# Input tile by input tile instead of chunk by chunk, for the first two weight chunks of a stage

## The chip, the cores and the metric

One core of one Trainium2 chip runs the whole program. The metric is the device time of one launch in microseconds (us). PE is the matrix engine (TensorE), DVE the vector engine, ACT the scalar engine, POOL is GpSimd, SP issues transfers.

## The reference, cut to what matters

One inference step of a decoder trunk of two layers, for 512 prompt tokens and 8 sample tokens that share all weights. Layer 0 mixes tokens by sparse attention, layer 1 by a causal pooling. All of it is float32:

```
x <- LN(ALPHA*x + 0.5*SwiGLU_1(x));  x <- LN(ALPHA*x + mixer(x));  x <- LN(ALPHA*x + 0.5*SwiGLU_2(x))

def _layernorm(x, g, b):
    mu = jnp.mean(xf, axis=-1, keepdims=True)
    var = jnp.mean(jnp.square(xf - mu), axis=-1, keepdims=True)
    y = (xf - mu) * lax.rsqrt(var + LN_EPS) * g + b

def _swiglu(x, w_i, w_o):
    h = jnp.einsum('btd,df->btf', x, w_i)
    gate, up = h[..., :D_FF], h[..., D_FF:]
    return jnp.einsum('btf,fd->btd', jax.nn.silu(gate) * up, w_o)
```

D_MODEL is 1024 and D_FF is 2816. A projection (`x @ w_in`, 2120 columns) comes before the attention.

## The kernel before, in words

The activations stay in SBUF with the features on the partitions: `xf` is 8 tiles of 128 features by 520 tokens. The tokens are handled in two halves of 260 (`HT`, `cols(h)`). A matmul keeps float32 accuracy in three products: every operand is split into a rounded high part and the remainder, `xh` and `xl` for the activations, `w_hi` and `w_lo` for the weights, and the products are xh*w_hi, xh*w_lo and xl*w_hi.

The seven stages are, in order, `f0` (feed-forward), `pr` (projection and attention), `op` (output projection), `f1`, `f2` (feed-forward), `pl` (pooling mixer), `f3` (feed-forward). The weights come in chunks of 1 MB: 8 tiles of 128 input features (k) by two blocks of 128 output columns (m). SP loads a chunk into `w_raw`, ACT makes `w_hi` (L486), DVE makes `w_lo` (L1155); each has two buffers. PE multiplies in `products` (L770). Each chunk has four banks of PSUM, two blocks m by two halves h: even chunks have banks 0 to 3, odd ones 4 to 7.

Five stages begin with `two_chunks`: f0, pr, f1, f2 and f3. It runs chunk 0 and chunk 1 for the first half of the tokens, then both for the second half. For one half and chunk, `products` first goes over the 8 tiles of `xh` with w_hi and w_lo (8 x 2 x 2 = 32 matmuls), then over the 8 tiles of `xl` with w_hi (16 matmuls). So a half has 2 x 48 = 96 matmuls. Chunk 0 waits before each tile of `xh` and each tile of `xl` for the semaphores `s_xh` and `s_x`; chunk 1 finds them all there.

Each engine runs its own list of instructions in order. What comes before `two_chunks` (except in f0) is the layer norm of the stage before, in `tail`. For the half h: PE sums with a matrix of means (`stats`, L813, six float32 matmuls, each of which the trace shows as two), ACT copies the mean (L499) and squares it (L500), DVE makes the variance and its reciprocal (L1170 to L1174), ACT takes the root (L504), DVE subtracts and multiplies tile by tile (L1181, L1187). Then `affine` on ACT writes per tile `xh` (L517) and then `xf` (L522), and POOL writes `xl` = xf - xh (L1765). `stats` of half 0 runs in the stage before. `stats` of half 1 is the function `left`, which the next stage gets as `middle_0`: it runs in the middle of the first 32 matmuls of chunk 0, at k = 4. All of the layer norm of half 1, and with it `xh` and `xl` for the second half of `two_chunks`, follows from it.

In f0 there is no layer norm ahead: all tiles of `xh` and `xl` come from the loaded input (ACT L720, POOL L1747), and `left` is None.

Of the kernel before, what the change touches and what calls it, by code (L numbers as in the profile page):

```python
# [18 lines left out]
KD = D // P  # L19
# [3 lines left out]
HT = TOK // 2  # L23
# [79 lines left out]
def trunk_kernel(nc, a, outs, stages):  # L103
    ctx = ExitStack()
    with ctx:
        def sem(name):
            return ctx.enter_context(nc.semaphore(name))
# [4 lines left out]
        def at(name, shape, dt=F32, offset=None):  # L112
            size = int(np.prod(shape[1:])) * (2 if dt == BF16 else 4)
            if offset is None:
                offset = top[0]
                top[0] += -(-size // 64) * 64
            return nc.alloc_sbuf_tensor_at(name, shape, dt, offset=offset)
# [3 lines left out]
        xh = at("xh", [P, KD, TOK], F32R)  # L121
        xl = at("xl", [P, KD, TOK], F32R)
# [3 lines left out]
        w_hi = at("w_hi", [P, 2, CHUNK], F32R)  # L126
        w_lo = at("w_lo", [P, 2, CHUNK], F32R)
# [27 lines left out]
        ps = ctx.enter_context(nc.psum_tensor("ps", [P, 8, 512], F32))  # L155
# [95 lines left out]
        def cols(h):  # L251
            return slice(h * HT, (h + 1) * HT)
# [10 lines left out]
        s_hi = sem("s_hi")  # L263
        s_lo = sem("s_lo")
        s_used = sem("s_used")
        s_free = sem("s_free")
# [12 lines left out]
        s_xh = sem("s_xh")  # L279
        s_xf = sem("s_xf")  # L280
        s_x = sem("s_x")
# [199 lines left out]
        def _(act):  # L481
# [47 lines left out]
            def proj(name):  # L529
                st = plan[name]  # L530
                act.dma_start(rope[:], a["c_rope"]).then_inc(s_rope_in, 16)
                act.wait_ge(s_kept, 32)
                act.wait_ge(s_stat, 2)
                act.dma_start(kidx[:], keys_dram.rearrange("n h (t d) -> (h t) n d", d=IDX_DIM)).then_inc(s_pages, 16)
                for li, (kind, g, _) in enumerate(PROJ):
                    if 1 <= li < len(PROJ) - 1:
                        if PROJ[li + 1][0] == "ki":
                            act.wait_ge(s_kiw, 16)
                        split_hi(st.chunk + li + 1)
                    act.wait_ge(s_used, 2 + st.chunk + li + 1)  # L540
                    for m, x in enumerate(rotated(li)):
                        nc.scalar.activation(halves(x), ps[:, 4 * (li % 2) + 2 * m:4 * (li % 2) + 2 * m + 2, 0:HT],
                                             ACT.Copy).then_inc(s_praw, 1)
# [208 lines left out]
        def _(pe):  # L752
            def products(c, nk, bank, hi, lo, first, last, m_cols=(P, P), before_hi=None, before_lo=None, middle=None,
                         only=(0, 1)):

                wh = w_hi[:, c % 2, 0:nk * 256].rearrange("p (k u c) -> p k u c", k=nk, u=2)
                wl = w_lo[:, c % 2, 0:nk * 256].rearrange("p (k u c) -> p k u c", k=nk, u=2)
                for x, before, ws in ((hi, before_hi, (wh, wl)), (lo, before_lo, (wh,))):  # L760
                    for k in range(nk):
                        if before is not None:
                            before(k)
                        if middle is not None and x is hi and k == nk // 2:
                            middle()
                        for m in range(2):
                            mc = m_cols[m]
                            for w in ws:
                                for h in only:
                                    mm = nc.tensor.matmul(ps[0:mc, bank + 2 * m + h, 0:HT], w[:, k, m, 0:mc],  # L770
                                                          x(k)[:, h * HT:(h + 1) * HT],
                                                          start=first and k == 0 and w is wh and x is hi,
                                                          stop=last and k == nk - 1 and x is lo)
                if 1 in only:
                    mm.then_inc(s_used, 1)
                return mm

            def first_x(st, h):

                return 0 if st.x == KD else st.x - 2 * KD + KD * h  # L780

            def two_chunks(st, middle_0, middle_1):

                for h in range(2):
                    for j in range(2):
                        if h == 0:
                            pe.wait_ge(s_lo, st.chunk + j + 3)
                            pe.wait_ge(s_free, 2 * (st.group + j) + 2)
                        products(st.chunk + j, KD, 4 * j, x_hi, x_lo, True, True,
                                 before_hi=(lambda k: pe.wait_ge(s_xh, first_x(st, h) + k + 1)) if j == 0 else None,  # L790
                                 before_lo=(lambda k: pe.wait_ge(s_x, first_x(st, h) + k + 1)) if j == 0 else None,
                                 middle=middle_0 if (h, j) == (0, 0) else middle_1 if (h, j) == (1, 1) else None, only=(h,))

            def x_hi(k):
                return xh[:, k, :]
# [20 lines left out]
            def ffn(name, left):  # L816

                st = plan[name]
                two_chunks(st, left, None)
                with pe.Fori(0, KF // 2 - 1) as i:  # L820
                    for j in (2, 3):
# [38 lines left out]
            def proj(name, left):  # L860
                st = plan[name]
                two_chunks(st, left, lambda: rotate(0))
                for li, (kind, g, _) in enumerate(PROJ):
                    if li < 2:
                        continue
                    c = st.chunk + li
                    pe.wait_ge(s_lo, c + 3)
                    pe.wait_ge(s_free, 2 * (st.group + li) + 2)
                    products(c, KD, 4 * (li % 2), x_hi, x_lo, True, True,
                             m_cols=(P, IDX_HEADS) if kind == "ki" else (P, P), middle=lambda: rotate(li - 1))  # L870
# [927 lines left out]
```

## Time and profile before

| what | value |
|---|---|
| time, median of 3 runs | 2199.44 us (2195.97 to 2200.57) |
| the profiled execution's own time | 2196.03 us |
| its span | 2194.2 us |
| PE busy | 1994.8 us, 91% of the span |
| DVE, ACT, POOL busy | 874.2, 597.8, 466.6 us |
| mean granted clock of PE | 0.936 of full speed |
| share of PE in the chain that ended last | 78% |

The span is what the profiler saw of the program; the time holds 1.8 us around it. PE is busy nearly everywhere but in the attention (about 540 to 860 us) and at the seams between stages. The seams that this change touches begin at 416 us (pr), 910 us (f1), 1302 us (f2) and 1775 us (f3); f0 begins its matmuls at 31.85 us.

### The profile page before, as it was taken

The page shows a single profiled execution, that of the slowest core. Times are in us where ns is not written, and L with a number is a line of the kernel's source. Part 1 is how long each engine was busy: PE and PEld are TensorE (multiplying, and loading weights), DVE is VectorE, ACT ScalarE, POOL GpSimd, SP SyncE. Part 2 cuts the span into 40 slices and gives each one's busy share as a digit, 9 for nine tenths or more (in the row PEclk, how much of TensorE's full clock was granted, in tenths as well). Part 3 has the DMA queues.
Part 4 walks back from the last instruction along what each step waited for, and adds up shares of the span by engine and source line. Part 5 has one row for each costly group of instructions (what it writes and reads, how often), then busy time and mean ns, then how long its engine had stood idle before and what let it go on. Part 6 is the DMA issues. An engine that isn't in the chain of part 4 may idle for free.

```text
span 2194.2 us, 36231 instructions
## 1 busy us (share of the span) xinstructions
PE 1994.8 (91%) x15486; PEld 1906.1 (87%) x15486; DVE 874.2 (40%) x1228; ACT 597.8 (27%) x837; POOL 466.6 (21%) x408
## 2 busy tenths in 40 slices
PE   6999999999957677999999999999999379999996
PEld 5999999999645456899999989999998369999996
DVE  2333322543686622533332244333224653333223
ACT  2222122421214241522222133122123452122123
POOL 2211121300000063511111232111121651111120
PEclk9999999999559798999999999999999689999998
DMA  5453322251000032233332232332230123323321
GB/s 168 139 168 96 96 87 87 74 157 39 23 0 1 1 87 68 77 96 88 84 96 87 92 92 78 96 89 83 91 106 30 51 69 96 96 83 89 98 77 39
DMA packets 258364, 179.55 MB, mean 82 GB/s; under 512 B 10806, under 2 KB 254782, under 8 KB 257757
## 3 DMA queue, kind: packets, MB, share of 16 engines
q1 hardware_dynamic: 248368, 153.71, 24.0%
q10 hardware_dynamic: 7797, 11.98, 1.7%
q0 software_dynamic: 2112, 12.59, 1.6%
q8 instruction: 67, 1.10, 0.2%
q14 instruction: 20, 0.16, 0.0%
HBM read 169.57 MB, written 8.08 MB: 81 GB/s over the span
## 4 chain that ended last, share of the span: by engine, by line
PE 78%; DVE 6%; issue 6%; ACT 3%; POOL 3%; another core or an unknown queue 1%; DMA 1%; ACTq 0%; POOLq 0%; DVEq 0%
PE ps L770 74%; PE ps L813 2%; PE ps L905 1%; DVE iwork L1310 1%; DVE best L1307 1%; ACT w_hi L486 1%; DVE w_lo L1155 1%; POOL diag L1706 1%; DVE xf L1181 1%; POOL sum_sq L1650 1%; DVE xf L1187 1%; POOL sum_z L1648 1%; ACT xf L522 1%; POOL k_sel L1696 1%
## 5 line engine op out<-in xcount | busy, mean ns | idle before, releaser
L770 PE MATMUL ps<-xh,w_hi 128*128 128x260 f32 x3264 | 684.7, 286 | 39.3 <-ACT xh L517 17.1
L770 PE MATMUL ps<-xh,w_lo 128*128 128x260 f32 x3264 | 677.2, 284 | 0.0
L1155 DVE TENSOR_TENSOR w_lo<-w_raw,w_hi 128x2048 fp32r<-128x2048 f32 (+2 forms) x153 | 441.0, 2883 | 442.5 <-ACT w_hi L486 442.5
L770 PEld LDWEIGHTS ps<-xh,w_hi 128*128 128x128 f32 x3264 | 519.4, 190 | 45.7 <-issue 26.6
L770 PEld LDWEIGHTS ps<-xh,w_lo 128*128 128x128 f32 x3264 | 519.8, 190 | 0.7
L770 PE MATMUL ps<-xl,w_hi 128*128 128x260 f32 x3264 | 411.7, 283 | 1.3 <-POOL xl L1734 1.3
L770 PEld LDWEIGHTS ps<-xl,w_hi 128*128 128x128 f32 x3264 | 399.6, 188 | 2.0 <-POOL xl L1734 1.5
L486 ACT CAST w_hi<-w_raw 128x2048 fp32r<-128x2048 f32 (+2 forms) x153 | 282.0, 1844 | 274.1 <-PE ps L770 262.9
L770 PE MATMUL ps<-hh,w_hi 128*128 128x260 f32 x1408 | 293.0, 283 | 0.0
L770 PE MATMUL ps<-hh,w_lo 128*128 128x260 f32 x1408 | 291.4, 282 | 0.0
L1580 DVE TENSOR_TENSOR hid<-silu_g,ps 128x520 f32<-128x520 f32 x88 | 61.3, 696 | 547.4 <-ACT silu_g L683 514.8
L683 ACT ACTIVATE silu_g<-ps 128x520 f32<-128x520 f32 x88 | 53.3, 605 | 758.5 <-PE ps L770 758.5
L770 PEld LDWEIGHTS ps<-hh,w_lo 128*128 128x128 f32 x1408 | 224.1, 188 | 0.1
L770 PEld LDWEIGHTS ps<-hh,w_hi 128*128 128x128 f32 x1408 | 223.9, 188 | 0.1
L1658 POOL CAST hh<-hid 128x520 f32 (+1 forms) x88 | 54.7, 621 | 787.9 <-DVE hid L1580 787.9
L770 PE MATMUL ps<-hl,w_hi 128*128 128x260 f32 x1408 | 177.5, 282 | 0.0
L770 PEld LDWEIGHTS ps<-hl,w_hi 128*128 128x128 f32 x1408 | 172.1, 188 | 0.0
L1660 POOL TENSOR_TENSOR hl<-hid,hh 128x520 f32 (+1 forms) x88 | 115.6, 1314 | 14.2 <-POOL hh L1658 14.1
L1648 POOL TENSOR_TENSOR sum_z<-sum_z,xf 128x520 f32<-128x520 f32 x36 | 58.3, 1619 | 200.3 <-DVE xf L1163 196.6
L1765 POOL TENSOR_TENSOR xl<-xf,xh 128x260 fp32r<-128x260 f32 x64 | 70.5, 1119 | 100.5 <-ACT xf L522 100.1
L1706 POOL TENSOR_TENSOR diag<-const,row_inv 128x512 f32<-128x512 f32 x16 | 16.7, 1042 | 336.3 <-DVE row_inv L1498 335.9
L970 PE MATMUL ps<-kd,q_t 64*128 64x512 f32 (+3 forms) x128 | 41.1, 609 | 31.6 <-DVE row_max L1438 31.6
(243 smaller groups left out, 1373.1 us busy)
## 6 DMA issues: line engine op xcount, KB each, us to landing
w_raw<-in_ffn_wi_dram SPq DMA_DIRECT2D x176, 512.0 KB
w_raw<-in_ffn_wo_dram SPq DMA_DIRECT2D x32, 1024.0 KB
w_raw<-in_ffn_wo_dram SPq DMA_DIRECT2D x16, 768.0 KB
w_raw<-in_attn_w_in_dram SPq DMA_DIRECT2D x8, 1024.0 KB
keys_scratch<-key_half POOLq DMA_DIRECT2D x2, 2048.0 KB, 7.9
w_raw<-in_attn_w_o_dram SPq DMA_DIRECT2D x4, 1024.0 KB
x_in<-in_x_prompt_dram ACTq DMA_DIRECT2D x1, 2048.0 KB
out_dram<-y_out ACTq DMA_DIRECT2D x4, 512.0 KB
```

The lines of the kernel that those rows point to most:

```text
L486: nc.scalar.copy(w_hi[:, c % 2, 0:n], w_raw[:, c % 2, 0:n]).then_inc(s_hi, 1)
L683: nc.scalar.activation(halves(silu_g[:, j % 2, :]), ps[:, 4 * (j % 2):4 * (j % 2) + 2, 0:HT], ACT.Silu).then_inc(s_silu, 1)
L770: mm = nc.tensor.matmul(ps[0:mc, bank + 2 * m + h, 0:HT], w[:, k, m, 0:mc], x(k)[:, h * HT:(h + 1) * HT], start=first and k == 0 and w is ...
L813: mm = nc.tensor.matmul(ps[:, 2 * q + h, 0:HT], mean_ones, x[:, cols(h)], start=n == 0, stop=n == 2)
L970: nc.tensor.matmul(ps[:, H % 2, 0:(i + 1) * P], q_t[64 * e:64 * e + 64, h // 2, i * P:(i + 1) * P], kd[64 * e:64 * e + 64, g, 0:(i + 1) * ...
L1155: nc.vector.tensor_tensor(w_lo[:, c % 2, 0:n], w_raw[:, c % 2, 0:n], w_hi[:, c % 2, 0:n].bitcast(F32), ALU.subtract).then_inc(s_lo, 1)
L1580: nc.vector.tensor_tensor(halves(hid[:, j % 2, :]), halves(silu_g[:, j % 2, :]), ps[:, b + 2:b + 4, 0:HT], ALU.mult).then_inc(s_free, 2)
L1648: nc.gpsimd.tensor_tensor(sum_z[:], sum_z[:], xf[:, d, :], ALU.add).then_inc(s_sum, 1)
L1658: nc.gpsimd.tensor_copy(hh_ij, hid[:, j:j + 1, :]).then_inc(s_hh, 1)
L1660: nc.gpsimd.tensor_tensor(hl_ij, hid[:, j:j + 1, :], hh_ij.bitcast(F32), ALU.subtract).then_inc(s_hl, 1)
L1706: nc.gpsimd.tensor_tensor(diag[:, B % 2], ident.unsqueeze(1).broadcast_to([P, 4, P]), row_inv[:, B % 2, :].unsqueeze(2).broadcast_to([P, 4 ...
L1765: nc.gpsimd.tensor_tensor(xl[:, d, cols(h)], xf[:, d, cols(h)], xh[:, d, cols(h)].bitcast(F32), ALU.subtract).then_inc(s_x, 1)
```

## The change

`two_chunks` no longer calls `products` for the first half of the tokens, but a new function `first_half`. It goes over the input tiles: for each k it multiplies `xh` with w_hi and w_lo of chunk 0 and with w_hi of chunk 1 (6 matmuls), then the `xl` of the tile before with w_hi of both chunks (4 matmuls). w_lo of chunk 1 comes after all tiles (16 matmuls). The second half of the tokens is as before. `left` is called at the same k = 4, after the six `xh` matmuls of that tile.

```
-                for h in range(2):
-                    for j in range(2):
-                        if h == 0:
-                            pe.wait_ge(s_lo, st.chunk + j + 3)
-                            pe.wait_ge(s_free, 2 * (st.group + j) + 2)
-                        products(st.chunk + j, KD, 4 * j, x_hi, x_lo, True, True,
-                                 before_hi=(lambda k: pe.wait_ge(s_xh, first_x(st, h) + k + 1)) if j == 0 else None,
-                                 before_lo=(lambda k: pe.wait_ge(s_x, first_x(st, h) + k + 1)) if j == 0 else None,
-                                 middle=middle_0 if (h, j) == (0, 0) else middle_1 if (h, j) == (1, 1) else None, only=(h,))
+            def first_half(st, middle):
+                view = "p (k u c) -> p k u c"
+                wh = [w_hi[:, (st.chunk + j) % 2, :].rearrange(view, k=KD, u=2) for j in range(2)]
+                wl = [w_lo[:, (st.chunk + j) % 2, :].rearrange(view, k=KD, u=2) for j in range(2)]
+
+                def tile(j, w, x, k, start, stop):
+                    for m in range(2):
+                        nc.tensor.matmul(ps[:, 4 * j + 2 * m, 0:HT], w[j][:, k, m, :], x[:, k, cols(0)], start=start, stop=stop)
+
+                pe.wait_ge(s_lo, st.chunk + 3)
+                pe.wait_ge(s_free, 2 * (st.group + 1) + 2)
+                for k in range(KD + 1):
+                    if k < KD:
+                        pe.wait_ge(s_xh, first_x(st, 0) + k + 1)
+                        tile(0, wh, xh, k, k == 0, False)
+                        tile(0, wl, xh, k, False, False)
+                        if k == 0:
+                            pe.wait_ge(s_hi, st.chunk + 2)
+                        tile(1, wh, xh, k, k == 0, False)
+                    if k == KD // 2 and middle is not None:
+                        middle()
+                    if k >= 1:
+                        pe.wait_ge(s_x, first_x(st, 0) + k)
+                        tile(0, wh, xl, k - 1, False, k == KD)
+                        tile(1, wh, xl, k - 1, False, False)
+                pe.wait_ge(s_lo, st.chunk + 4)
+                for k in range(KD):
+                    tile(1, wl, xh, k, False, k == KD - 1)
+
+                first_half(st, middle_0)
+                for j in range(2):
+                    products(st.chunk + j, KD, 4 * j, x_hi, x_lo, True, True,
+                             before_hi=(lambda k: pe.wait_ge(s_xh, first_x(st, 1) + k + 1)) if j == 0 else None,
+                             before_lo=(lambda k: pe.wait_ge(s_x, first_x(st, 1) + k + 1)) if j == 0 else None,
+                             middle=middle_1 if j == 1 else None, only=(1,))
```

Only PE's list changes. Its first rows of stage pr before (a row is an instruction or several alike, L770 is the matmul of `products`; in brackets the semaphores that it waits for):

```order
L770 MATMUL ps<-xh,w_hi 128x260 [waits s_xh,s_free,s_lo]
L770 MATMUL ps<-xh,w_lo 128x260
L770 MATMUL ps<-xh,w_hi 128x260
L770 MATMUL ps<-xh,w_lo 128x260
L770 MATMUL ps<-xh,w_hi 128x260 [waits s_xh]
```

The first rows of the same stage in the changed kernel (L791 is the matmul of `first_half`), up to the first tile of `xl`:

```order
L791 MATMUL ps<-xh,w_hi 128x260 [waits s_xh,s_free,s_lo]
L791 MATMUL ps<-xh,w_hi 128x260
L791 MATMUL ps<-xh,w_lo 128x260 x2
L791 MATMUL ps<-xh,w_hi 128x260 [waits s_hi]
L791 MATMUL ps<-xh,w_hi 128x260
L791 MATMUL ps<-xh,w_hi 128x260 [waits s_xh]
L791 MATMUL ps<-xh,w_hi 128x260
L791 MATMUL ps<-xh,w_lo 128x260 x2
L791 MATMUL ps<-xh,w_hi 128x260 x2
L791 MATMUL ps<-xl,w_hi 128x260 [waits s_x]
L791 MATMUL ps<-xl,w_hi 128x260 x3
```

The first wait for `s_x` stands after 12 matmuls now; before, it stood after 32 matmuls and the six of `stats`. The second place is `stats` of half 1 in the same stage. Before, from tile k = 3 on (L813 is `stats`):

```order
L770 MATMUL ps<-xh,w_hi 128x260 [waits s_xh]
L770 MATMUL ps<-xh,w_lo 128x260
L770 MATMUL ps<-xh,w_hi 128x260
L770 MATMUL ps<-xh,w_lo 128x260
L813 MATMUL ps<-sum_z,const 128x260 [waits s_sum,s_xh]
L813 MATMUL ps<-xf,const 128x260 [waits s_free] x2
L813 MATMUL ps<-sum_sq,const 128x260
L813 MATMUL ps<-silu_g,const 128x260 [waits s_sq] x2
L770 MATMUL ps<-xh,w_hi 128x260
```

In the changed kernel, from the `xl` matmuls behind tile k = 3 on (L841 is `stats` there):

```order
L791 MATMUL ps<-xl,w_hi 128x260 [waits s_x]
L791 MATMUL ps<-xl,w_hi 128x260 x3
L791 MATMUL ps<-xh,w_hi 128x260 [waits s_xh]
L791 MATMUL ps<-xh,w_hi 128x260
L791 MATMUL ps<-xh,w_lo 128x260 x2
L791 MATMUL ps<-xh,w_hi 128x260 x2
L841 MATMUL ps<-sum_z,const 128x260 [waits s_sum]
L841 MATMUL ps<-xf,const 128x260 [waits s_free] x2
L841 MATMUL ps<-sum_sq,const 128x260
L841 MATMUL ps<-silu_g,const 128x260 [waits s_sq] x2
```

Before, 16 matmuls stand ahead of `stats`, and no wait for `xl`; now 42 stand ahead of it (6 + 10 + 10 + 10 + 6), and three waits for `xl`.

## Rows read from the trace of the kernel before

**Rows 1.** Page, costliest groups: busy us, mean ns, idle before and its releaser.
```profile
L770 PE MATMUL ps<-xh,w_hi 128*128 128x260 f32 x3264 | 684.7, 286 | 39.3 <-ACT xh L517 17.1
```
**Rows 2.** Waits of PE at four seams: 410 to 425, 905 to 920, 1297 to 1312, 1769 to 1784 us.
```profile
PE ps L770 <- ACT xh L517: 3.0, 2, 2.6
...
PE ps L770 <- ACT xh L517: 3.6, 3, 2.6
...
PE ps L770 <- ACT xh L517: 3.7, 3, 2.6
...
PE ps L770 <- ACT xh L517: 6.6, 2, 6.2
```
**Rows 3.** Timeline of PE at the start of pr: start us, duration us.
```profile
416.45 0.56 PE L770 MATMUL ps<-xh,w_hi 128*128 128x260 f32 x1 [2.64 <-ACT xh L517]
...
417.02 0.42 PE L770 MATMUL ps<-xh,w_hi 128*128 128x260 f32 x1
417.23 0.42 PE L770 MATMUL ps<-xh,w_lo 128*128 128x260 f32 x1
```
**Rows 4.** Timeline of POOL: the first `xl` tile at each seam, and all eight in pr.
```profile
416.88 5.96 POOL L1765 TENSOR_TENSOR xl<-xf,xh 128x260 fp32r<-128x260 f32 x1 [29.09 <-ACT xf L522]
...
416.88 10.91 POOL L1765 TENSOR_TENSOR xl<-xf,xh 128x260 fp32r<-128x260 f32 x8 [29.09 <-ACT xf L522]
...
910.39 5.96 POOL L1765 TENSOR_TENSOR xl<-xf,xh 128x260 fp32r<-128x260 f32 x1 [9.85 <-ACT xf L522]
...
1302.34 5.96 POOL L1765 TENSOR_TENSOR xl<-xf,xh 128x260 fp32r<-128x260 f32 x1 [29.09 <-ACT xf L522]
...
1775.23 5.61 POOL L1765 TENSOR_TENSOR xl<-xf,xh 128x260 fp32r<-128x260 f32 x1 [11.91 <-ACT xf L522]
```
**Rows 5.** Timeline of DVE in pr: the last multiplications of half 0 and what follows.
```profile
419.28 0.76 DVE L1187 TENSOR_TENSOR xf<-xf,hid 128x260 f32<-128x260 f32 x2
419.96 2.29 DVE L1155 TENSOR_TENSOR w_lo<-w_raw,w_hi 128x2048 fp32r<-128x2048 f32 x1
```
**Rows 6.** Timeline of PE: `stats` at full clock with its end, then the first matmul after `stats` at each seam.
```profile
402.88 0.60 PE L813 MATMUL ps<-sum_z,const 128*128 128x260 f32 x2
...
405.32 0.47 PE L770 MATMUL ps<-hh,w_hi 128*128 128x260 f32 x1
...
424.62 0.48 PE L770 MATMUL ps<-xh,w_hi 128*128 128x260 f32 x1
...
918.83 0.48 PE L770 MATMUL ps<-xh,w_hi 128*128 128x260 f32 x1
...
1311.08 0.47 PE L770 MATMUL ps<-xh,w_hi 128*128 128x260 f32 x1
...
1783.05 0.47 PE L770 MATMUL ps<-xh,w_hi 128*128 128x260 f32 x1
```
**Rows 7.** Timeline of PE in pr: the last group of the first half, and the first matmul of the second.
```profile
432.49 2.08 PE L770 MATMUL ps<-xl,w_hi 128*128 128x260 f32 x16
434.41 0.29 PE L770 MATMUL ps<-xh,w_hi 128*128 128x260 f32 x1
```
**Rows 8.** Timelines: in pr ACT's last `xh` of half 1 and PE's first matmul with it; the same matmul in f2.
```profile
437.12 0.60 ACT L517 ACTIVATE xh<-xf,lnp 128x260 fp32r<-128x260 f32 x1
...
437.77 0.39 PE L770 MATMUL ps<-xh,w_hi 128*128 128x260 f32 x1
...
1324.63 0.39 PE L770 MATMUL ps<-xh,w_hi 128*128 128x260 f32 x1 [0.24 <-ACT xh L517]
```
**Rows 9.** PE in stretches: us, busy (instructions), granted clock, share of DMA, GB/s.
```profile
409.70:416.40 6.70, 4.11 (x35) 1.00 0.23 48
416.50:423.20 6.70, 6.33 (x21) 0.50 0.23 34
423.40:430.00 6.60, 6.60 (x52) 1.00 0.50 157
911.50:918.10 6.60, 5.81 (x18) 0.50 0.13 34
918.30:925.00 6.70, 6.70 (x54) 1.00 0.41 116
```
**Rows 10.** Timeline of f0's start: POOL's eight `xl` tiles, and PE's first matmul of the stage.
```profile
25.44 10.07 POOL L1747 TENSOR_TENSOR xl<-xf,xh 128x520 fp32r<-128x520 f32 x8 [8.49 <-ACT xh L720]
...
31.85 0.39 PE L770 MATMUL ps<-xh,w_hi 128*128 128x260 f32 x1 [0.85 <-DVE xf L1621]
```

## The prediction

> **What bounds the kernel now.** I read the page first. PE is busy for 91% of the span and is 78% of the chain that ended last, so what counts is the time in which PE does nothing or runs slowly. The costliest group shows where its matmuls on `xh` stood idle: 39.3 us in all, 17.1 of them until ACT had written `xh` [rows 1]. Then the waits at the four seams with a layer norm. They are 3.0, 3.6, 3.7 and 6.6 us, and the longest wait of each (2.6, 2.6, 2.6, 6.2) is the one before the first tile [rows 2]. A new order of the matmuls can't shorten that one: at that time there is no tile. What is left between the tiles is 0.4 + 1.0 + 1.1 + 0.4 = 2.9 us over the four seams. That is all that an order "as the tiles come" can fill.
>
> Then I looked at when the other inputs come. POOL's first `xl` tile takes 5.96 us (5.61 in f3), while all eight take 10.91, so that the other seven take (10.91 - 5.96) / 7 = 0.71 each [rows 4]. The first begins at 416.88 and ends at 422.84. In that time DVE multiplies tiles and then makes `w_lo`, until 419.96 + 2.29 = 422.25 [rows 5]; POOL gets going as DVE stops. In the kernel before nobody feels this, because PE comes to `xl` only after `stats`, 424.62 us, and 16 matmuls more [rows 6].
>
> Last, the clock. From 416.5 to 423.2 it is granted at 0.50 (1.2 GHz), from 423.4 on at 1.00 (2.4 GHz); in f1 it is 0.50 from 911.5 to 918.1 [rows 9]. Ahead of the fall in pr PE had stood still for 2.64 us [rows 3].
>
> **The prices.** At full clock 16 matmuls take 434.41 - 432.49 = 1.92 us, 0.12 each [rows 7]. At half clock one takes 0.21 [rows 3]. `stats` at full clock takes 405.32 - 402.88 = 2.44 us [rows 6].
>
> **The change part by part.** No instruction is added or removed but semaphore waits: both orders have 96 matmuls in the first half. What changes is what stands behind what.
>
> *The wait for the first xl.* In pr PE starts at 416.45 and does the 12 matmuls of tiles 0 and 1 at 0.21 each, to 419.0. Then it waits for `xl` tile 0 until 422.84, about 3.8 us. Behind it on PE's list stand the `xh` tiles 2 to 7, which ACT goes on delivering, and `stats`. Later `xl` tiles come each 0.71 us and PE needs at least 10 x 0.12 = 1.2 us for a tile, so there is one such wait per seam.
>
> *The delay of stats, at full clock.* From the first `xl` on, 4 + 10 + 10 + 6 = 30 matmuls (3.60 us) and `stats` (2.44) make 6.04 us. So `stats` would end at these times, against the first matmul after it in the kernel before [rows 4, 6]:
> - pr: 422.84 + 6.04 = 428.88 against 424.62, 4.26 later
> - f1: 916.35 + 6.04 = 922.39 against 918.83, 3.56 later
> - f2: 1308.30 + 6.04 = 1314.34 against 1311.08, 3.26 later
> - f3: 1780.84 + 6.04 = 1786.88 against 1783.05, 3.83 later
>
> The sum is 14.9 us. The 2.9 us of small waits are inside these numbers, since they are taken from absolute times.
>
> *Does it reach the end?* Yes, by the last `xh` of half 1. In pr ACT ends it at 437.12 + 0.60 = 437.72 and PE takes it up at 437.77, and in f2 PE already waits 0.24 us for it [rows 8]. All of the second layer norm hangs on `stats`, by a fixed chain on ACT and DVE, so this tile comes as much later as `stats` does, and there is at most 0.1 us of slack. PE itself would reach the second half at 428.88 + 54 x 0.12 = 435.4, only 1 us later than now (434.41 [rows 7]); it then waits inside the second half. Where 28 matmuls took it to tile 7 by 438.7, the tile comes at 437.72 + 4.3 = 442.0: 3.3 us of new waiting.
>
> *The clock after the first stall.* The clock is at half when PE gets its `xl`, and it now has done little before. Bounds: it could be full at once (0), or come back only as long after PE's restart as before, 416.45 to 423.3 or 6.8 us [rows 3, 9], which costs half of that, 3.4. It is work at half clock in all of these rows after a stall, so I take 4.5 us at half, a cost of 2.2 per seam.
>
> *The clock in the second half.* 3.3 us of waiting in some 6.6 us. Before, the stretch with 4.11 us busy of 6.70 was followed by the fall [rows 9]. This is as thin, but the waits are short ones between tiles. Bounds 0 and 3.4, as above; I take 1.5 per seam.
>
> *At nothing.* Chunk 1's w_lo is wanted later than before and w_hi of chunk 1 is written by ACT ahead of `xh`. The wait for both chunks' banks at the start is for DVE work that lies ahead of the normalising. In f0, POOL's tiles end 1.26 us apart from 26.7 on, the last at 35.5; PE starts at 31.85 and comes to `xl` tile j at 31.85 + (12 + 10 j) x 0.12 = 33.3 + 1.2 j, always later [rows 10]. If POOL were 7 us later there, it would be another such stall. The second half's own order, SP's and POOL's queues are as before. Behind the seams the feed-forward stages have PE busy all the time and pr leads into a chain of dependent work, so nothing there gives the delay back.
>
> **The sum:** 14.9 + 4 x 2.2 + 4 x 1.5 = 29.7 us. Against the profiled execution's own 2196.0 that is 2225.7. The median of the runs is 3.4 us higher, 2199.4, so I say 2229. With both clock terms at nothing it is 14.9 us (2214), with both at their upper bound 14.9 + 27.2 = 42.1 (2241.5).
>
> **The rivals.**
> - *Not slower: the xl tiles are there in time.* The wait at the 13th matmul decides: if POOL ended its first tile by 419.0, in 2.1 us instead of 5.96, PE would run through, and the 2.9 us between the tiles would be filled: 2196.5. For it: POOL's later tiles take 0.71 us. Against it: DVE's work of that time is the same in both kernels and POOL's first tile is long at all four seams [rows 4]. Even so `stats` would stand behind 26 more matmuls. Chance 0.07.
> - *The delay is hidden in the second half.* If the layer norm of half 1 had slack, only the end of the first half would count. After `stats` come 54 matmuls (6.5 us) instead of 80 (9.6), so 3.1 of each delay is made good and 14.9 - 12.4 = 2.5 us are left, with the first clock term 11.3: 2211. Against it stands the 0.24 us wait in f2 [rows 8]. Chance 0.07.
> - *The alternation of banks slows PE.* In the new order each matmul goes to another bank than the one before. If that held PE to 0.21 a matmul, 96 x 0.09 x 5 stages = 43 us would come on top: 2272. Against it: the 16 `xl` matmuls of [rows 7] alternate between two banks at 0.12 each. Chance 0.03. The Trainium skill, page "TensorE: Matmul & The Clock Gate", section "A second HAM failure mode: psum-queue depth-cycling", speaks for it: it tells of a kernel that cycled through PSUM banks and whose clock swung between the two levels by small pauses. By that rule the time would be this rival's; the trace's alternating matmuls at full clock don't bear it out.
>
> **How the numbers follow.** The forecast, a stall for `xl` and a late `stats` that both reach the end, has 0.83. It spans 2214 to 2241.5; I take 2210 to 2243, which lets the hidden case in as well and leaves out the first and the third rival. A measurement of this kernel can tell about 0.2%, 4.4 us, from no change. Faster by more than that: 0.02, a part of the first rival. Within: 0.06, the rest of it and a little of the second. Slower: 0.92.
>
> **What would show it right or wrong.** Right: at pr, f1, f2 and f3 the waits of PE show `xl` <- POOL (L1765) with 3.5 to 5 us each, a new line; small waits for `xh` in the first half go, and new ones of about 3 us per seam for `xh` come in the second half; `stats` ends 3.3 to 8 us later after the first `xh` than before; the half-clock stretch after each seam is longer or comes twice, and the mean granted clock falls below 0.936. POOL's first `xl` still takes near 6 us, and f0 is unchanged. Wrong: no wait for `xl`, or one under 2 us; or the waits as told but the second half unchanged in its end, which is the second rival; or steady matmuls in `first_half` at more than 0.12 us with the clock at 1.00, the third.

## The result, and the profile after

| | kernel before | changed kernel |
|---|---|---|
| median of 5 runs | 2199.44 us | 2224.31 us |
| lowest to highest | 2195.35 to 2200.57 | 2216.84 to 2224.49 |
| span of the profiled execution | 2194.2 us | 2222.5 us |
| mean granted clock of PE | 0.936 | 0.928 |

The changed kernel is slower: ratio 1.0106, 95% interval 1.0085 to 1.0128, which is 23.3 us (18.7 to 28.2) on 2199.4. The ratio is taken over all runs and not from the two medians, which lie 24.9 us apart. The forecast was 2229, 29.7 us above before, with a range of 2210 to 2243.

The waits of PE in the changed kernel, over the whole program (us in total, times, the longest); L791 is the matmul of `first_half`, L770 that of `products`:

```profile
PE ps L791 <- POOL xl L1793: 14.9, 4, 4.5
...
PE ps L791 <- ACT xh L517: 14.1, 4, 6.2
...
PE ps L770 <- ACT xh L517: 7.3, 16, 0.6
```

The first line is new: four waits for `xl`, one per seam, 14.9 us. The second is the wait before the first tile, 2.6 + 2.6 + 2.6 + 6.2, which was there before; the small ones between the tiles of half 0 [rows 2] are gone. The third is new but for one wait of 0.24 us that the kernel before had in f2 [rows 8]: 16 small waits for `xh` in the second half.

The timeline of PE at the start of pr in the changed kernel, from the first matmul to `stats` (L841), the first matmul after it, and the last wait of the second half; it answers to [rows 3] and [rows 6 to 8]:

```profile
418.65 0.59 PE L791 MATMUL ps<-xh,w_hi 128*128 128x260 f32 x2 [2.64 <-ACT xh L517]
...
420.76 0.64 PE L791 MATMUL ps<-xh,w_hi 128*128 128x260 f32 x2
425.08 1.24 PE L791 MATMUL ps<-xl,w_hi 128*128 128x260 f32 x4 [3.68 <-POOL xl L1793]
...
430.57 0.60 PE L841 MATMUL ps<-sum_z,const 128*128 128x260 f32 x2
...
432.32 1.04 PE L841 MATMUL ps<-silu_g,const 128*128 128x260 f32 x4
433.01 0.84 PE L791 MATMUL ps<-xl,w_hi 128*128 128x260 f32 x4
...
446.11 0.39 PE L770 MATMUL ps<-xh,w_hi 128*128 128x260 f32 x1 [0.24 <-ACT xh L517]
```

After 12 matmuls PE stands still for 3.68 us. `stats` begins 11.9 us after the seam's first matmul; before it was 4.5. The next matmul after it comes 14.4 us after the first, before 8.2. And the last `xh` of half 1 is taken up 446.11 - 418.65 = 27.5 us after the first matmul, where it was 437.77 - 416.45 = 21.3 [rows 3, 8].

POOL and DVE at that time in the changed kernel:

```profile
419.07 5.95 POOL L1793 TENSOR_TENSOR xl<-xf,xh 128x260 fp32r<-128x260 f32 x1 [29.10 <-ACT xf L522]
```
```profile
422.15 2.28 DVE L1183 TENSOR_TENSOR w_lo<-w_raw,w_hi 128x2048 fp32r<-128x2048 f32 x1
```

POOL's first tile ends at 425.02, DVE's `w_lo` at 424.43: as before [rows 4, 5], to 0.01 us. Only its reader has come closer.

PE in four stretches of this seam (us, busy, granted clock), to be held against [rows 9]:

```profile
418.70:425.00 6.30, 2.70 (x12) 0.51 0.24 34
425.10:428.50 3.40, 3.40 (x16) 0.50 0.87 263
428.90:438.00 9.10, 9.10 (x67) 0.99 0.01 4
438.00:447.00 9.00, 7.16 (x51) 1.00 0.14 36
```

In pr the clock is at half through the stall and for some 3.5 us after it, then full. It stays full in the second half, though PE waits there. In f1 the first 12 matmuls still ran at full clock, in 1.9 us, so that the stall is the longest of the four, 4.5 us, and the clock is at half for 5.9 us after it.

**Where the 28.3 us between the two spans lie.** The first matmul of each seam comes at 418.65, 921.91, 1320.12 and 1797.57, before at 416.45, 909.96, 1301.91 and 1774.80 (the latter three from the same timeline as [rows 3]). So the lag is 2.2 us at pr, 12.0 at f1, 18.2 at f2, 22.8 at f3 and 28.3 at the end. f1 adds 6.3, f2 with pl 4.6, f3 5.5. In pr the first matmul of the attention scores comes at 558.9 instead of 551.2, a lag of 7.7: the seam adds 5.5, and the attention behind it another 4.2. The four seams are 21.9 us of the 28.3; the 2.2 ahead of pr and the 4.2 in the attention are taken up below. In a second profile of the kernel before, the stretch from pr to f1 is 3.2 us shorter than in the first, the other three are the same to within 0.7 us.

### The profile page after: what moved, and what is told of

The parts are those of the page before. It is cut to its first block, busy times and chain, and to the rows that moved or that the text cites. A ratio compares the mean times of both kernels' runs of the same rounds, so it can differ in the third digit from the quotient of the medians.

```text
span 2222.5 us, 36222 instructions
## 1 busy us (share of the span) xinstructions
PE 2011.7 (91%) x15486; PEld 1918.9 (86%) x15486; DVE 873.4 (39%) x1228; ACT 597.4 (27%) x837; POOL 465.5 (21%) x408
## 3 DMA queue, kind: packets, MB, share of 16 engines
q1 hardware_dynamic: 248368, 153.71, 23.7%
## 4 chain that ended last, share of the span: by engine, by line
PE 77%; DVE 7%; issue 7%; POOL 4%; ACT 3%; DMA 1%; ACTq 0%; POOLq 0%; DVEq 0%
PE ps L770 71%; PE ps L791 2%; PE ps L841 1%; PE ps L933 1%; DVE iwork L1338 1%; DVE best L1335 1%; POOL xl L1793 1%; DVE xf L1209 1%; DVE xf L1215 1%; ACT w_hi L486 1%; DVE w_lo L1183 1%; POOL diag L1734 1%; POOL sum_sq L1678 1%; DVE hid L1202 1%; POOL sum_z L1676 1%
## 5 line engine op out<-in xcount | busy, mean ns | idle before, releaser
L770 PE MATMUL ps<-xh,w_hi 128*128 128x260 f32 (+1 forms) x3104 | 641.9, 285 | 28.5 <-DVE w_lo L1183 16.9
L770 PE MATMUL ps<-xh,w_lo 128*128 128x260 f32 (+1 forms) x3104 | 635.3, 283 | 0.0
L770 PEld LDWEIGHTS ps<-xh,w_hi 128*128 128x128 f32 (+1 forms) x3104 | 487.1, 189 | 35.6 <-DVE w_lo L1183 11.6
L770 PEld LDWEIGHTS ps<-xh,w_lo 128*128 128x128 f32 (+1 forms) x3104 | 487.0, 189 | 0.5
L770 PE MATMUL ps<-xl,w_hi 128*128 128x260 f32 (+1 forms) x3104 | 390.9, 283 | 1.0 <-POOL xl L1762 1.0
L770 PEld LDWEIGHTS ps<-xl,w_hi 128*128 128x128 f32 (+1 forms) x3104 | 379.7, 189 | 1.7 <-POOL xl L1762 1.2
L770 PE MATMUL ps<-hh,w_hi 128*128 128x260 f32 x1408 | 293.0, 283 | 0.0
L770 PE MATMUL ps<-hh,w_lo 128*128 128x260 f32 x1408 | 291.6, 282 | 0.0
L770 PEld LDWEIGHTS ps<-hh,w_lo 128*128 128x128 f32 x1408 | 224.2, 188 | 0.1
L770 PEld LDWEIGHTS ps<-hh,w_hi 128*128 128x128 f32 x1408 | 223.9, 188 | 0.1
L770 PE MATMUL ps<-hl,w_hi 128*128 128x260 f32 x1408 | 177.5, 282 | 0.0
L770 PEld LDWEIGHTS ps<-hl,w_hi 128*128 128x128 f32 x1408 | 172.1, 189 | 0.0
L1688 POOL TENSOR_TENSOR hl<-hid,hh 128x520 f32 (+1 forms) x88 | 115.5, 1312 | 14.3 <-POOL hh L1686 14.1
```

Source lines behind the costliest of these rows:

```text
L1688: nc.gpsimd.tensor_tensor(hl_ij, hid[:, j:j + 1, :], hh_ij.bitcast(F32), ALU.subtract).then_inc(s_hl, 1)
```

## The experiments

One number tells most of them: how long after a seam's first matmul POOL begins the first `xl` tile of half 1. It stands for the start of the second half's input, and can be read from two rows of each timeline. In us:

| kernel | pr | f1 | f2 | f3 | sum |
|---|---|---|---|---|---|
| before | 14.01 | 14.72 | 15.42 | 14.37 | 58.5 |
| before, second profile | 14.72 | 15.42 | 15.41 | 14.35 | 59.9 |
| changed | 20.19 | 21.04 | 19.92 | 20.02 | 81.2 |
| stats late, old order | 18.33 | 18.32 | 18.31 | 17.99 | 73.0 |
| new order in f0 alone | 14.71 | 15.40 | 14.75 | 13.68 | 58.5 |
| changed, POOL ahead of DVE | 16.21 | 17.74 | 18.97 | 18.34 | 71.3 |
| xl five behind, stats at tile 4 | 14.02 | 15.79 | 14.01 | 13.68 | 57.5 |
| stats early, old order | 13.54 | 14.01 | 13.55 | 13.68 | 54.8 |
| stats early, new order | 13.55 | 13.54 | 13.56 | 13.70 | 54.4 |
| xl four behind, stats early | 13.57 | 13.55 | 13.55 | 13.69 | 54.4 |
| the same, second profile | 13.56 | 13.57 | 13.56 | 13.68 | 54.4 |
| the same, moments early | 13.26 | 12.56 | 13.26 | 13.06 | 52.1 |

Against the mean of the two profiles of before, 59.2, the changed kernel is 22.0 us late. The ratios of small effects have to be read with this table: the kernel with the new order in f0 alone has the old order at all four seams, and its ratio is 0.9985. So a ratio of 0.998 to 0.999 doesn't show by itself that an edit at the seams gains anything.

### stats early, in the new order

```
-                    if k == KD // 2 and middle is not None:
+                    if k == 1 and middle is not None:
                         middle()
```

> The changed kernel with stats of half 1 behind tile 1's xh matmuls (12 matmuls ahead of it) instead of behind tile 4's (42). Theory A (the loss is the late layer norm of half 1, caused by stats standing behind the wait for the first xl): stats starts about 2.5 us after the first matmul of a seam, fills the stall, and ends no later than in the kernel before; the xh tiles of half 1 come no later than before, the wait for the first xl falls from 3.1-4.5 us to under 2. Time 2197 to 2208, ratio 0.999 to 1.004. Rival B (the stall costs its own length on PE, whatever stats does): the part of the stall that stats doesn't fill, at most 1.5 us a seam, is left: 2200 to 2206, so this run alone doesn't part it from A. Rival C (the order of the matmuls, a bank change at each one, is what costs): still 2218 to 2226.

Measured: 2197.86 us against 2198.58, ratio 0.9985 (0.9970 to 1.0000). Its waits of PE for `xl`:

```profile
PE ps L791 <- POOL xl L1793: 4.4, 3, 1.9
```

The seam of pr in that kernel:

```profile
417.76 0.48 PE L791 MATMUL ps<-xh,w_hi 128*128 128x260 f32 x2 [2.64 <-ACT xh L517]
...
419.49 0.60 PE L841 MATMUL ps<-sum_z,const 128*128 128x260 f32 x2
...
421.24 1.04 PE L841 MATMUL ps<-silu_g,const 128*128 128x260 f32 x4
424.19 0.75 PE L791 MATMUL ps<-xl,w_hi 128*128 128x260 f32 x4 [1.91 <-POOL xl L1793]
```

`stats` now begins 1.7 us after the first matmul (2.7 at most at the other seams) and lies inside the time in which PE would wait. The whole loss is gone, with the order of the 96 matmuls untouched. Rival C, the order itself as the cost, falls. A and B aren't parted by it, as said.

### stats late, in the old order

In the kernel before, `stats` of half 1 is called in chunk 0's loop over `xl`, at k = 5, behind 32 + 10 = 42 matmuls:

```
-                        if middle is not None and x is hi and k == nk // 2:
+                        if middle is not None and (x is hi and k == nk // 2 if late is None else x is lo and k == late):
                             middle()
```

> The kernel before, its order kept, with stats of half 1 moved from behind 16 matmuls to behind 42 (inside chunk 0's xl loop), where all xl tiles it needs are there: no stall for xl. Theory A: stats ends 26 x 0.12 to 26 x 0.21 = 3.1 to 5.5 us later less the gaps that it no longer waits in, PE waits 2 to 4 us per seam for xh of half 1, and the time is 10 to 18 us above before, 2209 to 2218. Rival B (only the stall costs): no wait for xl, so 2197 to 2203, as before. Rival C (bank changes): as before, 2197 to 2203.

Measured: 2211.68 us, ratio 1.0063 (1.0044 to 1.0083), which is 13.9 us. The waits of PE for `xh`, which were 17.1 us in 11 pieces [rows 1]:

```profile
PE ps L770 <- ACT xh L517: 22.2, 26, 6.2
```

`stats` of pr in that kernel, and the last wait in the second half:

```profile
419.16 0.36 PE L770 MATMUL ps<-xh,w_hi 128*128 128x260 f32 x1 [2.64 <-ACT xh L517]
...
429.12 0.71 PE L813 MATMUL ps<-sum_z,const 128*128 128x260 f32 x2 [0.19 <-POOL xl L1765]
...
443.91 0.39 PE L770 MATMUL ps<-xh,w_hi 128*128 128x260 f32 x1 [0.25 <-ACT xh L517]
```

There is hardly a wait for `xl` (0.19 us), and yet `stats` begins 10.0 us after the first matmul instead of 4.5, half 1's first `xl` comes 13.8 us later over the four seams (73.0 against 59.2), and the time follows. So 42 matmuls ahead of `stats` cost by themselves, without any stall. Rival B, only the stall costs, falls. About 14 of the 23 us are the place of `stats` behind 42 matmuls; the remaining 9 or so, by difference, are what the stall adds to it. The waits for `xh` in the second half are 1.0 to 1.8 us per seam, shorter than the 2 to 4 that were expected.

### the new order in f0 alone

`two_chunks` chooses `first_half` only where `st.x == KD`, else the old code.

> The new order in stage f0 alone, the old one in pr, f1, f2 and f3. All xl tiles are ahead of PE there and no stats stands in it. Theory A: no wait for xl, the time as before, 2196 to 2202; the 2.1 us that f0 took longer in the changed kernel's profile was the clock and comes or goes from run to run. Rival C: 96 matmuls take longer at full clock too, 0.14 us instead of 0.12 each, 2 us more than before in every profile.

Measured: 2195.07 us, ratio 0.9985 (0.9971 to 0.9999). No wait for `xl` in f0. From PE's first matmul of f0 to the first Silu on ACT it took 19.8 us in this profile. Nothing is lost by the order where all inputs are there. Whether the 3 us are a gain I leave open: no row shows where it would come from, and the interval ends at 0.9999.

### the kernel before, once more

> The kernel before once more, for a second profile. Theory A on the scatter: f0's matmuls begin at the same time (31.9 us), but the moment at which they reach 0.12 us each varies by some us from execution to execution, and so do stretches of the attention; the four seams lie where they lay to within 2 us each. Rival C: the first 20 matmuls of f0 always take 0.12 us in this order.

Measured: 2195.83 us in one run, span 2194.0. The first matmuls of f0 in this second profile of the old order, and the first Silu:

```profile
32.23 0.58 PE L770 MATMUL ps<-xh,w_hi 128*128 128x260 f32 x1 [0.85 <-DVE xf L1621]
...
33.05 0.42 PE L770 MATMUL ps<-xh,w_lo 128*128 128x260 f32 x1
33.27 0.42 PE L770 MATMUL ps<-xh,w_hi 128*128 128x260 f32 x1
...
52.00 0.60 ACT L683 ACTIVATE silu_g<-ps 128x520 f32<-128x520 f32 x1 [17.63 <-PE ps L770]
```

They are 0.22 us apart, as at half clock, until 37.2, and from the first matmul to the Silu it is 19.8 us. In the profile that the forecast was made from it was 17.55, and in the changed kernel 19.6. So the changed kernel's lag of 2.2 us at pr comes and goes with the execution, and not with the order. The seam of pr began at 419.08 here, later than in the changed kernel (418.65), and 2.6 us later than in the first profile, where 2 at most had been expected.

### the changed kernel, with POOL ahead of DVE

DVE waits for POOL's first two `xl` tiles before it makes w_lo of chunk 1, which `first_half` wants only at its end:

```
                 if nxt is not None:
+                    if nxt != plan["pl"].chunk:
+                        follow = [s for s in plan.values() if s.chunk == nxt][0]
+                        dve.wait_ge(s_x, follow.x - 2 * KD + 2)
                     split_lo(nxt + 1)
```

> The changed kernel, in which DVE waits for POOL's first two xl tiles before it makes w_lo of chunk 1 (L1183), at the four seams. If POOL's first tile is long because DVE's work holds it up, it now ends about 2.2 us sooner after the seam's first matmul (some 3.8 us long instead of 5.95), PE's wait for xl falls from 3.1-4.5 to 1-2.4 us, stats ends some 2 us sooner per seam, and the time falls by 6 to 10 us against the changed kernel: 2212 to 2218. w_lo is wanted only at the end of the first half, 10 us later, so making it later costs nothing. Rival D (POOL's first tile is long by itself, a start-up cost of the engine after its long idle time): it stays at 5.95 us, PE's wait too, and the time stays at 2218 to 2226.

Measured: 2209.49 us, ratio to the kernel before 1.0045 (1.0031 to 1.0059). The waits of PE for `xl`, POOL's first tile in pr, and DVE's `w_lo` there:

```profile
PE ps L791 <- POOL xl L1796: 6.1, 4, 2.3
```
```profile
418.34 3.75 POOL L1796 TENSOR_TENSOR xl<-xf,xh 128x260 fp32r<-128x260 f32 x1 [29.09 <-ACT xf L522]
```
```profile
422.82 2.82 DVE L1183 TENSOR_TENSOR w_lo<-w_raw,w_hi 128x2048 fp32r<-128x2048 f32 x1 [1.32 <-POOL xl L1796]
```

The tile takes 3.75 us instead of 5.95, shorter by the 2.2 us for which DVE's `w_lo` had followed the normalising; it still ends only as DVE pauses. And the long tile has moved: the fourth one, which fell beside `w_lo`, now takes 2.79 us, and ends at 426.24, just after `w_lo` at 425.64.

```profile
423.45 2.79 POOL L1796 TENSOR_TENSOR xl<-xf,xh 128x260 fp32r<-128x260 f32 x1
```

Rival D, a start-up cost of POOL, falls. The Trainium skill says the same of the cause: page "GPSIMD Engine Reference", section "1. Specifications", has POOL's SBUF interfaces shared with the vector engine, in contention with DVE instructions that have two SBUF inputs, as these have. The trace agrees: the first tile takes 5.95 us beside them in the changed kernel, while the median of all 64 tiles there is 0.75.

PE's waits for `xl` fell by 8.8 us, as expected. The median lies 14.8 us under that of the changed kernel and below the 2212 to 2218 expected. By the two ratios to the kernel before, 1.0106 and 1.0045, the fall is 13.4 us, and by their intervals it may be 8 to 19. In the profile `stats` ends 9.9 us sooner over the four seams, and the first `xl` of half 1 comes 9.9 sooner too. That is within this range; nothing shows that the rest is this edit's.

### xl five tiles behind

`stats` stays at tile 4, but the xl matmuls follow five tiles behind the xh ones instead of one, so that 30 matmuls and no wait for `xl` are ahead of `stats`. Here and in the next but one the edit is the lag of the `xl` tiles:

```
-                for k in range(KD + 1):
+                for k in range(KD + 5):
...
-                    if k >= 1:
-                        pe.wait_ge(s_x, first_x(st, 0) + k)
-                        tile(0, wh, xl, k - 1, False, k == KD)
-                        tile(1, wh, xl, k - 1, False, False)
+                    if k >= 5:
+                        pe.wait_ge(s_x, first_x(st, 0) + k - 4)
+                        tile(0, wh, xl, k - 5, False, k == KD + 4)
+                        tile(1, wh, xl, k - 5, False, False)
```

> The changed kernel with stats where it is (tile 4) but the xl matmuls five tiles behind, so that no wait for xl stands ahead of stats and 30 matmuls do instead of 42. Theory A: no wait for xl; stats starts 30 x 0.21 = 6.3 us (at half clock) after the seam's first matmul, against 4.5 in the kernel before, so 1 to 2.5 us late; waits for xh of half 1 of 1 to 2 us per seam; time 3 to 9 us above before: 2202 to 2208. Rival B (only a stall for xl costs): as before, 2196 to 2200.

Measured: 2194.18 us, ratio 0.9988 (0.9979 to 0.9997). That is under the 2202 to 2208 that theory A gave, and just below the 2196 to 2200 of B, which another run has ruled out. The seam of pr:

```profile
419.31 0.49 PE L791 MATMUL ps<-xh,w_hi 128*128 128x260 f32 x2 [2.64 <-ACT xh L517]
...
424.77 0.60 PE L841 MATMUL ps<-sum_z,const 128*128 128x260 f32 x2
...
427.21 0.59 PE L791 MATMUL ps<-xh,w_hi 128*128 128x260 f32 x2
```

and the two stretches of it:

```profile
419.40:423.20 3.80, 3.80 (x18) 0.57 0.40 55
423.50:427.20 3.70, 3.70 (x24) 1.00 0.23 39
```

In pr `stats` does begin later, 5.5 us after the first matmul instead of 4.5, but it ends sooner, at 7.9 instead of 8.2 to 8.4. All twelve of its matmuls run at full clock, in 2.44 us; in the kernel before part of them ran at half and they took 3.64. I had priced the 30 matmuls at half clock throughout and had forgotten that `stats` runs at half in the kernel before. Here PE, with no gap between its matmuls, had the full clock back about 4 us after the first. In f2 and f3 `stats` ended sooner too, at 8.2 and 7.9 against 8.9 to 9.2 and 8.2. In f1 it was otherwise: PE waited 0.5 us after 12 matmuls, the clock was at half until past 918, `stats` ended 10.0 us after the first matmul, 1.0 to 1.1 later than in the kernel before, and half 1's first `xl` came at 15.79, later too. So theory A holds in its cause, at the seam that lost as at the three that won: when `stats` ends, half 1 follows (57.5 against 59.2 in all). Its estimate of that time was wrong.

### stats early, in the old order

`stats` behind 8 matmuls (k = 2) in chunk 0.

> The kernel before, order kept, with stats of half 1 behind 8 matmuls (k = 2) instead of 16. Theory A: stats starts some 2 us sooner, and the small waits for xh of half 1 (0.2 us in f2, f3) go; ACT's moments still wait for the end of its affine tiles of half 0, so the chain gains under 1 us per seam, and PE has hardly a wait in the second half to lose: 2193 to 2199, ratio 0.996 to 1.000, perhaps not to be told from no change.

Measured: 2193.82 us, ratio 0.9985 (0.9976 to 0.9994). The first `xl` of half 1 comes 4.4 us sooner over the four seams, and no wait for `xh` is left in the second half. By the ratio that is a gain of about 3 us without the new order at all. The rows at the seams bear it out, the ratio alone doesn't, since the run with the new order in f0 alone has the same.

### xl four tiles behind and stats early, and moments early on top

The lag is 4 and `stats` stands at tile 1. This kernel was run twice:

> The changed kernel's order with stats behind tile 1 and the xl matmuls four tiles behind the xh ones instead of one, so that PE meets the first xl after 30 matmuls and stats. Theory A: no wait for xl any more (4.4 us over three seams in the profile with stats early), the small waits for xh of half 0 are filled; what comes last then is xh of half 1 with waits of under 1.5 us per seam. Gain against stats early alone up to 4 us: 2190 to 2198. If the gain is under 1 us, the second half's xh tiles are the bound and took it.

> The kernel with xl four tiles behind and stats early once more, for the comparison on the same chip: 2186 to 2192, ratio to the kernel before 0.995 to 0.9975; half 1's first xl tile again 13.5 to 13.7 us after the seam's first matmul.

Measured: 2187.69 us, ratio 0.9961 (0.9948 to 0.9974), of 5 runs; and 2196.61 us, ratio 0.9977 (0.9959 to 0.9996), of 12 runs, against 2200.69 of the kernel before. The second median lies outside what I had expected, and so, by little, does its ratio. No wait for `xl` in a seam is left in either profile; for `xh` of half 1 there are, in the first:

```profile
PE ps L770 <- ACT xh L517: 2.4, 8, 0.5
```

By both ratios it is faster than the kernel before, by 5 to 9 us, and by some 30 us than the changed one.

In the last kernel ACT takes the moments of half 1 ahead of its tiles 6 and 7 of half 0:

```
-                affine(n, st, 0, split, order, windows, ahead, KD)
+                early_at = KD if windows or not split else 6
+                affine(n, st, 0, split, order, windows, ahead, early_at)
                 moments(st, 1)
+                affine(n, st, 0, split, order, windows, early_at, KD)
                 root(st, 1)
```

> The kernel with xl four tiles behind and stats early, and on ACT the moments of half 1 ahead of the affine tiles 6 and 7 of half 0 instead of behind them. If the layer norm of half 1 is what comes last (waits for xh of half 1 of 2.4 us in all in that kernel's profile, half 1's first xl tile begun 13.55 us after the seam's first matmul at all four seams), that tile begins 1 to 2 us sooner, 11.5 to 12.6 us, the 2.4 us of waits go, and the time falls by 1 to 3 us: 2184 to 2188. If PE is the bound by then, the tile comes sooner and the time stays.

Measured: 2198.05 us, ratio 0.9986 (0.9971 to 1.0002): no gain over the kernel without it, which had 0.9977 in the same comparison. Its first `xl` tile of half 1 begins 13.3, 12.6, 13.3 and 13.1 us after the first matmul, 0.3 to 1.0 sooner instead of 1 to 2, and the waits for `xh` in the second half are 3.3 us, not gone. What took the rest wasn't tried.

## Why the prediction was right

**The waits for the first `xl`: right.** One per seam was forecast, 3.8 us in pr, 3.5 to 5 in all. Measured: 3.7, 4.5, 3.5 and 3.1 us. f3 is a little under the range: POOL's first tile is the short one there [rows 4], and the 12 matmuls ahead of the wait took 2.9 us at half clock where 2.5 were forecast.

**The delay of `stats`: right in sum and in its parts.** Forecast: 14.9 us at full clock and 8.8 us for the clock, 23.7. Measured from the seam's first matmul to the first one after `stats`: 14.4, 15.2, 14.1 and 14.2 us against 8.2, 8.9, 9.2 and 8.3, which is 23.4 us later. Behind the end of POOL's first tile the forecast had 6.04 us at full clock; measured are 8.0, 8.8, 7.7 and 8.2. The excess, 8.5 us, is the first clock term, forecast at 8.8, and what is left are the 14.9 of full clock. The old-order run shows that this place costs even without a stall.

**That it reaches the end: right.** Half 1's input is 22.0 us later over the four seams, the seams themselves are 21.9 us longer, and the time is 23.3 us longer. Moving `stats` alone removed it.

**The clock in the second half: wrong.** The forecast put 1.5 us on each seam for a second fall. The granted clock is 1.00 there, in pr over 9.0 us with 7.16 busy. The step that failed is the one from thin work to a slower clock. The forecast held the second half, 3.3 us of waiting in some 6.6, against the stretch ahead of pr with 4.11 us busy of 6.70, behind which the clock fell [rows 9], and called it as thin. The same stretch in the changed kernel:

```profile
439.70:446.10 6.40, 4.57 (x30) 1.00 0.08 12
```

The waiting itself came as forecast: PE takes 6.42 us from its first matmul of the second half to the last `xh` tile, at each of the four seams, for 28 matmuls that take 3.36 without a wait, so 3.1 us are lost. The waits that the profile lists are only 1.8 us of it, since the matmul behind each wait is slower as well (0.39 us against 0.28). But PE waits in four pieces of at most 0.65 us here, while the fall of the clock at the start of pr had one standstill of 2.64 us ahead of it. The granted clock stays at 1.00. What parts the two cases no run here shows. The term should have been nothing, and the sum would have been 23.7 instead of 29.7. That is 0.4 us from the 23.3 measured, while 29.7 lies above the interval of the measured difference, 18.7 to 28.2.

That the two profiled spans are 28.3 us apart, so near to 29.7, is luck: 6.4 of them are the 2.2 in f0 and the 4.2 in the attention, which the forecast had not in its sum.

**f0 at nothing: right,** by the run with the new order in f0 alone. **The rivals** fell as the rows had spoken. No `xl` was there in time; the delay wasn't hidden; and the matmuls of `first_half`, with a change of bank at each one, ran at full clock at 0.12 us each (in pr eight of them from 436.81 to 437.77), so the alternation costs nothing. The Trainium skill, page "TensorE: Matmul & The Clock Gate", section "A second HAM failure mode: psum-queue depth-cycling", which the forecast had named, tells of a clock that swings by small pauses in a kernel that cycles through PSUM banks. No run here shows this: in pr the granted clock is 0.99 from 428.9 to 438.0, with PE busy throughout.

## What to carry to other kernels

An order that takes each input "as it comes" must ask in which order the inputs of both kinds come: here the second input of the first tile came after the first input of the sixth, and a wait for it stood in front of everything else on the engine. Look for the small step in the middle of a dense stretch on which another engine's long chain hangs (here six matmuls of statistics), and count what stands ahead of it in matmuls and in waits; putting it first made the same new order harmless. And price a gap by what it leaves to fill: 2.9 us over four seams was all that this order could have won by itself.

## What the runs showed of the hardware that was not expected

**The granted clock in the rows missed a stretch at half clock.** In f0 the matmuls of the changed kernel are 0.22 us apart from 31.94 to about 36.5, and so they are in the second profile of the kernel before until 37.2, while the row of the changed kernel says full clock:

```profile
32.00:36.50 4.50, 4.50 (x21) 1.00 0.00 0
```

21 matmuls in 4.50 us are 0.21 each, as at the seams where the row says 0.50. In the first profile of the kernel before, the same window holds 38 matmuls, and its row says 1.00 as well. So the spacing of the matmuls is the surer sign. That the clock is what halved the rate in f0 is read from this spacing; no row says so.

**Executions of one kernel differ by more than many an edit.** From f0's first matmul to its first Silu it took 17.55 us in one profile of the kernel before and 19.8 in the other, and 18.8 to 20.3 in the profiles of the experiments. The stretch from the seam of pr to that of f1 took 487.0 us in one profile of the fastest kernel and 499.7 in the other, with half 1's first `xl` tile at the same distance from each seam's first matmul to within 0.02 us. The attention's second part in the two:

```profile
700.00:850.00 150.00, 93.56 (x641) 0.86 0.15 43
```
```profile
700.00:850.00 150.00, 99.30 (x634) 0.79 0.15 43
```

The first is of 2187.7 us, the second of a run of 2200.2. The thin, broken work of the attention gets the full clock for more or less of its time from execution to execution. The 4.2 us of the changed kernel's lag in the attention, which no edit touches, fit this: from 560 to 850 us the granted clock is 0.73 in the kernel before, and 0.69 in the changed one in the stretch that answers to it, 567.7 to 857.7. So does it that the same kernel shows 0.9961 once and 0.9977 the next time. Neither is shown by more than these profiles. For a change at the seams, the distance between two rows at the seam told more than the times.

**The dearest matmuls are those at half clock.** Behind 30 matmuls `stats` took 2.44 us at three seams and 3.4 at f1; behind 16, in the kernel before, it took 3.6 us or more at all four, since its float32 matmuls, which the trace shows as two each, fell in part into the half-clock stretch.
